# A hybrid decoder step on one core: the order and the queues of its first transfers

## The reference

```python
xn = rmsnorm(x, lp['norm1_g'])
u, q, k, v, qm, gates = jnp.split(xn @ lp['w_in'], split_at, axis=-1)
y_ssm, h_re, h_im = s5_scan(u, h0_re, h0_im, lp)          # diagonal state space, 32 groups
z = jax.nn.gelu(y_ssm)
z = z * jax.nn.sigmoid(z @ lp['w_glu'] + lp['b_glu'])
o_swa = ...                                               # window attention, 8 heads
o_mem = mem_attention(...)                                # cross attention to 256 tokens
merged = (g[:, :, 0] * (z @ lp['w_br_ssm']) + g[:, :, 1] * (o_swa @ lp['w_br_swa'])
          + g[:, :, 2] * (o_mem @ lp['w_br_mem']))
x = x + merged @ lp['w_out']
x = x + hier_moe(rmsnorm(x, lp['norm2_g']), lp)           # 32 experts, top 2 of one group
```

## Time and profile before

| | us |
|---|---|
| median of three executions | 860.25 (859.4 to 860.82) |
| profiled execution | 857.05 |
| its span, first to last instruction | 855.3 |
| TensorE busy (matmuls) | 798.1, 93% of the span |
| VectorE busy | 366.8, 43% |
| ScalarE busy | 211.8, 25% |
| GpSimd busy | 75.4, 9% |

### The profile page before, as it was taken

The page is one execution under the profiler, slowest core; times in us unless marked ns, Lnnn a source line. Parts: engine busy times, 40 slices in busy tenths (PEclk is TensorE's granted clock), DMA queues, the critical chain, the costliest instruction groups (busy, mean ns, idle before and its releaser), DMA issues. The chain is left out here.

```text
span 855.3 us, 11794 instructions
## 1 busy us (share of the span) xinstructions
PE 798.1 (93%) x4531; PEld 573.9 (67%) x4531; DVE 366.8 (43%) x854; ACT 211.8 (25%) x389; POOL 75.4 (9%) x105
## 2 busy tenths in 40 slices
PE   8999999999999999999999999999899987787874
PEld 7887887779888766678999998887333332332321
DVE  2697566662701156627815438446111111011017
ACT  2411400001331253427433233212111110110113
POOL 0100230000101101000000000002011101100000
PEclk9999999999999999999999999999999999999988
DMA  9651284121445615140026176139999999999957
GB/s 339 246 174 50 76 90 113 50 98 57 141 163 199 246 50 193 55 148 2 1 99 210 48 289 259 50 130 417 420 419 419 421 420 421 419 420 420 419 210 306
DMA packets 34551, 186.10 MB, mean 218 GB/s; under 512 B 5979, under 2 KB 6251, under 8 KB 17512
## 3 DMA queue, kind: packets, MB, share of 16 engines
q1 hardware_dynamic: 22288, 148.22, 43.7%
q0 software_dynamic: 11344, 35.24, 13.1%
q10 hardware_dynamic: 864, 1.88, 0.6%
HBM read 176.17 MB, written 17.22 MB: 226 GB/s over the span
## 5 line engine op out<-in xcount | busy, mean ns | idle before, releaser
L501 PE MATMUL ps<-sb 128*128 128x288 f32 (+15 forms) x3070 | 601.0, 426 | 46.7 <-DMA sb<-in_wexp 30.2
L501 PEld LDWEIGHTS ps<-sb 128*128 128x128 f32 (+7 forms) x3070 | 386.9, 166 | 234.0 <-issue 152.8
L501 PE MATMUL ps<-sr 128*128 128x288 f32 (+2 forms) x1056 | 157.6, 309 | 0.0
L501 PEld LDWEIGHTS ps<-sr 128*128 128x128 f32 x1056 | 146.5, 188 | 6.1 <-issue 0.4
L512 PEld LDWEIGHTS ps<-sb 128*128 128x128 f32 (+3 forms) x405 | 42.1, 140 | 32.6 <-issue 28.1
L2098 DVE SCALAR_TENSOR_TENSOR sb<-sb,ps 128x256 f32<-128x256 f32 x16 | 6.7, 421 | 125.8 <-ACT sb L1426 125.8
L1842 DVE TENSOR_TENSOR sr<-sb,sr 128x2048 fp32r<-128x2048 f32 (+2 forms) x25 | 45.0, 1818 | 28.9 <-ACT sr L1311 14.4
L512 PE MATMUL ps<-sb 128*128 128x128 f32 (+3 forms) x405 | 53.1, 270 | 2.6 <-issue 1.9
L2107 DVE COPY sb<-ps 128x1024 f32<-128x1024 f32 (+1 forms) x16 | 19.1, 1191 | 68.3 <-PE ps L501 68.3
L1128 ACT ACTIVATE sb<-ps 128x576 f32<-128x576 f32 (+4 forms) x29 | 22.9, 790 | 94.2 <-PE ps L501 66.9
L1830 DVE SCALAR_TENSOR_TENSOR sb<-sb,ps 128x576 f32<-128x576 f32 x24 | 18.0, 752 | 50.6 <-PE ps L501 50.6
(11 more groups left out here) (245 smaller groups left out, 417.2 us busy)
## 6 DMA issues: line engine op xcount, KB each, us to landing
sb<-in_wexp SPq DMA_DIRECT2D x96, 1024.0 KB, 28.1
sb<-in_wstream SPq DMA_DIRECT2D x33, 1024.0 KB, 4.9
sb<-in_mkT POOLq DMA_DIRECT2D x8, 512.0 KB, 7.4
sb<-in_mv POOLq DMA_DIRECT2D x8, 512.0 KB, 5.3
sb<-expert_rows SPq DMA_DIRECT2D x8, 512.0 KB, 7.8
sb<-in_x SPq DMA_DIRECT2D x4, 512.0 KB, 14.1
sb<-k_pad POOLq DMA_DIRECT2D x8, 256.0 KB, 10.5
sb<-in_x POOLq DMA_DIRECT2D x4, 512.0 KB, 10.4
```

The source lines that it names most:

```text
L501: return signed(nc.tensor.matmul(*a, **kw))
```

## The change

Three transfers change places, in three queues. SyncE's queue begins with x^T group 0 in place of the first weight quarter. ScalarE's queue begins with the first weight quarter, in place of the small constants and x^T group 0; the rest of it follows one place sooner. GpSimd's queue begins with the small constants, ahead of its wait for the memsets. Semaphores, sizes, addresses and all waits stay; no computing instruction changes.

```diff
@@ sync
-            first_block(0).then_inc(w0_ready[0], 16)
+            sp.dma_start(at(O_XG, (1, T)), xT[:, 0:T]).then_inc(ld_xT[0], 16)
             sp.dma_start(at(O_XG + T, (1, T)), xT[:, T:2 * T]).then_inc(ld_xT[4], 16)
             first_block(1).then_inc(w0_ready[1], 16)
@@ scalar
-            act.dma_start(at(O_SM, (1, N_SMALL)), small).then_inc(ld["small"], 16)
-            act.dma_start(at(O_XG, (1, T)), xT[:, 0:T]).then_inc(ld_xT[0], 16)
+            act.dma_start(at(O_W, (1, 512)), wstream[0][:, 0:512]).then_inc(w0_ready[0], 16)
             act.dma_start(at(O_XG + 2 * T, (1, 2 * T)), xT[:, 2 * T:4 * T]).then_inc(ld_xT[1], 16)
@@ gpsimd
+            pool.dma_start(at(O_SM, (1, N_SMALL)), small).then_inc(ld["small"], 16)
             pool.wait_ge(consts_set, 3)
             pool.dma_start(k_d[:, :, 0:112].rearrange("(a g) h c -> (g h) a c", g=8),
```

## The result

The changed kernel is slower. Its median over 20 executions is 863.64 us (861.73 to 866.38), the kernel before in the same rounds 860.55 us (857.46 to 865.29); the medians lie 3.1 us apart; the ratio is 1.0031, 95% interval 1.0019 to 1.0043. That is 0.3%, small but clear of noise. The forecast was 0.6 us faster, with a range from 858.7 to 862.0. Of the two rivals with a loss in them both came, together: the small constants land late on GpSimd's queue, and TensorE's clock is at its lower level behind the longer idle gap.

What follows compares the result with a forecast made beforehand. TensorE's start was taken to bound the kernel, carried unchanged to the end. A net gain of 0.6 us, with ScalarE's saved issue and the constants' move at zero, gave 860.25 - 0.6 = 859.65 us; range 858.7 to 862.0.

Steps and rivals of the forecast that it cites:

- the two rivals with a loss in them: Constants late on GpSimd's queue, 1.1 to 2.4 us lost, chance 0.22; TensorE's clock low, 2 us more, no separate chance.
- What bounds the kernel: Whole program hangs on TensorE's start at 7.05 us; a microsecond gained there is a microsecond at the end.
- Part 1: x^T group 0 first on SyncE's queue: lands at 5.5 to 5.7 us, first matmul gains 0.7 to 0.9 us.
- Part 2: Transfers behind the first: x^T group 1 lands at 7.4 us (6.9 to 7.8); net gain taken as 0.6 us.
- Part 3: ScalarE issues one transfer less and reaches its table load 0.45 us sooner, hidden: no cost, no gain.
- Part 4: Constants on GpSimd's queue: issued at 0.75 us, landing at 5.6 us (bounds 2.75 to 8.75), no cost.
- the rival had its price: Constants land late on GpSimd's queue, at 7.45 to 8.75 us; TensorE starts 1.1, 1.6 or 2.4 us later; chance 0.22.
- The clock: TensorE's start: earlier start at lower clock cuts gain to 0.3 us; longer idle gap adds 2 us; no separate chance.
- the late case: Constants land late on GpSimd's queue; TensorE's idle gap behind the warm-up grows from 1.93 to 3.0 us and more.
- the late rows: Trace rows of other transfers, 6.7, 7.2 and 8.0 us to landing, giving times of 861.3 to 862.6 us.

Runs made afterwards that it cites:

- small_third: Changed kernel, but the small constants on SyncE's queue behind its third transfer instead of on GpSimd's; 867.76 us against 862.24 for the kernel before, ratio 1.0074.
- small_pool: Kernel before with only the small constants moved from the head of ScalarE's queue to the head of GpSimd's; 863.14 us against 862.74, ratio 1.0009.
- swap: Kernel before with x^T group 0 first on SyncE's queue, first weight quarter second on ScalarE's behind the constants; 860.34 us, ratio 0.9977; again 860.47, 0.9983.
- pool_alone: Changed kernel with SyncE's and ScalarE's first transfers waiting until the constants have landed; one profiled execution, constants 2.3 us from issue to landing, span 860.8 us.
- pool_extra: Kernel before plus one more 79-KB transfer of the constants at the head of GpSimd's queue, into a place nothing reads; 863.19 us against 861.15, ratio 1.0015.
- after_look1: The changed kernel unaltered, run once more for another profile; no time or ratio of its own is given.
- before_again: The kernel before unaltered, run once more for a second profile; 861.81 us against 862.24, ratio 0.9996.

## Why the prediction was wrong

- **What bounds the kernel, and that the start is carried to the end:** right in the main. For the whole change the marks (2.9 us) and the first timed difference (3.1) agree, and `small_third`'s start 4.5 us later cost 5.5 us. It is not exact: `small_pool`'s mark is 2.7 us behind and its time 0.8 (2.2 at most), and the stretch at 610 us adds 1 to 4 us in some executions whatever the start.
- **Part 1, group 0 of x^T lands at 5.5 to 5.7 us:** the number is right, 5.6, but in part by luck. The sum had the constants' 81 kB moved by then, and they had not begun at 6.5 us; and in the swap, where they are moved, the group lands at 4.0. Bytes on the curve of another order don't give the landing to a tenth.
- **Part 2, group 1 lands at 7.4:** 7.6, inside its bounds. That wait never came to decide, since the start was later than all of it.
- **Part 3, ScalarE's earlier table load is worth nothing:** nothing in the traces speaks against it. The load stands at 3.40 instead of 4.42 us, and ScalarE then waits 3.64 us for the constants.
- **Part 4, the constants land at 5.6 us:** this is the step that failed. It had two terms. The issue on GpSimd's queue was taken at 0.75 us and is at 1.31: the row that shows the earliest time of this queue (k_pad, waiting for VectorE until 1.41) said nothing on 0.75, and I took the other queues' time for it. And the time to landing was taken from the row nearest in size (64 KB, 4.8 us) and is 7.0; the row nearest in place and moment, k_pad at 8.0, would have given 8.75, against the 8.3 that came. The reason given for 5.6, that the constants stand at the head of all queues, is what does not hold: they head their own, but are issued 0.56 us behind the first transfers of the others and behind 1442 kB of theirs. In its second part the prediction adds such bytes up for group 1, which is issued 0.12 us sooner than the constants were, and gets 7.4; for the constants it did not. `pool_alone` shows why size was the wrong measure: ahead of the others, 79 and 224 KB take 2.3 and 2.8 us, so most of such a time (4.7 of 7.0 us) is the company and not the transfer. The landing at 8.3 us was inside the bounds, and the rival had its price (2.4 us by k_pad's row, 1.85 measured), but a chance of 0.22 where the nearest row in place spoke for it.
- **The clock:** the rival named it, with 2 us for eight records more in the late case; that is about what it is in one execution (2.1 to 3.0 us). What was missed is that the kernel before pays 7 or 8 records in three profiles of four. The one profile at hand showed none. There was a hint: that execution took 857.05 us, 3.20 less than the median of the three timed ones, and the prediction carried this over as a constant. Against the medians the clock's part is 1.2 us.
- **The range** ended at 862.0 because it took the middle of the late rows without the clock on top, though the text had both in one sentence. Start 1.7 and clock 1.2 give 860.25 + 2.9 = 863.2; measured 863.64.
- **The rule of the Trainium skill** on issuing engines ("DMA: Bandwidth & Descriptors", "Issuing engines are not separate DMA queues": only the sequencer's time is saved) was worked out in the prediction to a gain of 0.43 us. Its part on sharing the same DMA engines agrees with the runs: 2.3 us for the constants alone, 7.0 beside the others. The gain does not come, and the measurement decides: the same 79 KB at the head of a queue landed 4.3 us after issue on ScalarE's, issued at 0.75, and 7.0 on GpSimd's, issued at 1.31. How much of that is the queue and how much the later issue behind the others' bytes, these rows don't part.
- **The other rule**, of "TensorE: Matmul & The Clock Gate", section "HAM oscillation", that the array falls back to half rate in waits for transfers, agrees with the profiles: 3.89 us of idling, then 0.50 of the clock. The prediction's remark that the array came out of 1.93 us of idling at the higher level held for that one profile: behind 2.07 to 2.37 us the three others show 7 or 8 records at the lower one.

The version that beats both kernels, by some 0.2%, is the swap without GpSimd: 0.9977 and 0.9983 of the kernel before in two sets of rounds, both intervals below 1.

## What to carry to other kernels

A transfer that gates the first instruction belongs at the head of a queue that is fast at the start; moving a small one to a free queue isn't free when the others open fire at the same moment, and its latency there is to be read from the row nearest in place and company, not in size, or from the bytes that the others have issued ahead of it. A later start of the bounding engine costs more than its own length when its clock falls in the gap: read the count of records in a window beside the busy share, and take more than one profile of the kernel before where this is in play. And when the last of several transfers is advanced, list all others with their landings: the next in line sets the gain.

## What the runs showed of the hardware

- A 79-KB transfer on GpSimd's queue took 2.3 us alone, 6.7 to 7.1 us when the two other queues had begun 0.56 us ahead of it with 1442 kB, and 6.0 us with 933 kB (`pool_extra`); in the changed kernel its first packet started more than 5.2 us behind the issue. The same transfer first on ScalarE's queue took 3.5 us (swap) or 4.3 to 4.5 (before).
- GpSimd's first transfer is issued at 1.31 us where ScalarE's and SyncE's are issued at 0.75.
- TensorE's level at the first real matmul differs between executions of one kernel: behind 1.93 to 2.37 us of idling 0, 8, 8 and 7 records ran at half rate, behind 3.76 to 4.19 us of it in the changed kernel 10 to 14. The gap's length alone does not set the count: the two profiles of the swap had 9 and 1 behind 1.75 and 1.77 us, `small_third` had 8 behind 6.54. In `after_look1`, and in `before_again`, `swap` and `pool_alone` too, the recorded clock says 1.00 in windows in which only 4 to 6 records pass in 2 us; the count is the safer sign.
- Two large transfers at the head of both hardware queues (changed kernel) landed at 5.6 and 5.7 us, but one large beside one small (swap) at 4.0 and 4.2, and the large one of before at 4.9. Why the swap's first landings are so much sooner than the bytes alone explain is not settled.
